# A two-layer transformer trunk in f32: index scores and attention logits as three rounded terms, and a reordered end

## The reference

```python
sc = einsum('bqhd,bsd->bqhs', qi, ki)              # 8 index heads of 64, one shared key
I = einsum('bqh,bqhs->bqs', wi * idx_scale, relu(sc))
vals, idx = lax.top_k(where(adm, I, -inf), 64)     # 64 keys for each query
logits = einsum('bqhd,bqkhd->bqhk', q, k[idx]) * 0.125
prob = softmax(where(valid, logits, -inf)); out = einsum(prob, v[idx])
```

## Time and profile before

| | |
|---|---|
| median of 3 runs (1175.69 to 1175.87) | 1175.69 us |
| profiled execution, own time | 1175.69 us |
| its span | 1173.9 us |
| TensorE busy | 99% |
| VectorE, ScalarE, GpSimd busy | 70%, 52%, 10% |
| TensorE's granted clock over the span | 0.998 |

### The profile page before, as it was taken

One profiled execution on the slowest core, in us unless ns is written; L12 is line 12 of the kernel. 1 busy time (PEld: TensorE's weight loads), 2 busy tenths in 40 slices (PEclk: granted clock), 3 DMA queues, 4 the chain that ended last, 5 costly groups with the idle time before them and its releaser, 6 DMA issues.

```text
span 1173.9 us, 24028 instructions
## 1 busy us (share of the span) xinstructions
PE 1166.0 (99%) x10518; PEld 1142.5 (97%) x10518; DVE 820.7 (70%) x936; ACT 610.0 (52%) x689; POOL 117.3 (10%) x130
## 2 busy tenths in 40 slices
PE   9999999999999999999999999999999999999998
PEld 9999999999999999999999999999899999999997
DVE  6866545697978766655786665458799787666556
ACT  6544445555745644444764443447466555444455
POOL 2000001011512000001110000100134020000011
PEclk9999999999999999999999999999999999999999
DMA  8655555545445555555546555554644456655551
GB/s 296 230 203 189 190 204 176 188 150 204 152 145 194 202 193 201 191 188 196 192 179 220 184 205 186 184 213 141 218 146 149 140 207 210 203 184 201 190 180 37
DMA packets 33528, 218.87 MB, mean 186 GB/s; under 512 B 5200, under 2 KB 6544, under 8 KB 7440
## 3 DMA queue, kind: packets, MB, share of 16 engines
q1 hardware_dynamic: 33424, 217.34, 53.5%
HBM read 216.15 MB, written 1.05 MB: 185 GB/s over the span
## 4 chain that ended last, share of the span: by engine, by line
PE 98%; DMA 1%; DVE 0%; ACT 0%; SPq 0%; DVEq 0%; issue 0%
PE psum L408 32%; PE psum L409 31%; PE psum L410 31%; PE psum L690 1%; PE psum L669 1%; DMA x_all<-in_x 1%; PE psum L542 0%; PE psum L603 0%; PE psum L653 0%; PE psum L724 0%; DVE gates L1795 0%; PE psum L638 0%; PE psum L735 0%; PE psum L758 0%; DVE hB_lo L1763 0%; PE psum L585 0%
## 5 line engine op out<-in xcount | busy, mean ns | idle before, releaser
L1303 DVE TENSOR_TENSOR w_lo<-raw,w_hi 128x2048 fp32r<-128x2048 f32 x200 | 457.9, 2293 | 218.7 <-ACT w_hi L903 218.5
L903 ACT ACTIVATE w_hi<-raw 128x2048 fp32r<-128x2048 f32 x201 | 385.2, 1916 | 352.2 <-PE psum L410 344.3
L408 PE MATMUL psum<-hA_hi,w_hi 128*128 128x256 f32 x1360 | 377.6, 278 | 0.0
L409 PE MATMUL psum<-hA_hi,w_lo 128*128 128x256 f32 x1360 | 375.7, 276 | 0.0
L410 PE MATMUL psum<-hA_lo,w_hi 128*128 128x256 f32 x1360 | 375.6, 276 | 0.0
L408 PEld LDWEIGHTS psum<-hA_hi,w_hi 128*128 128x128 f32 x1360 | 255.3, 188 | 2.7 <-issue 2.7
L409 PEld LDWEIGHTS psum<-hA_hi,w_lo 128*128 128x128 f32 x1360 | 255.3, 188 | 0.0
L410 PEld LDWEIGHTS psum<-hA_lo,w_hi 128*128 128x128 f32 x1360 | 255.3, 188 | 0.0
L408 PE MATMUL psum<-hB_hi,w_hi 128*128 128x256 f32 x832 | 229.9, 276 | 1.0 <-DVE w_lo L1771 1.0
L409 PE MATMUL psum<-hB_hi,w_lo 128*128 128x256 f32 x832 | 229.7, 276 | 0.0
L410 PE MATMUL psum<-hB_lo,w_hi 128*128 128x256 f32 x832 | 229.7, 276 | 0.0
(11 more groups left out here) (208 smaller groups left out, 1240.7 us busy)
## 6 DMA issues: line engine op xcount, KB each, us to landing
raw<-in_weights SPq DMA_DIRECT2D x203, 1024.0 KB, 4.9
raw<-in_weights SPq DMA_DIRECT2D x2, 512.0 KB, 6.2
out<-gates SPq DMA_DIRECT2D x4, 192.0 KB, 2.2
x_all<-in_x SPq DMA_DIRECT2D x1, 520.0 KB, 3.9
x_all<-in_x SPq DMA_DIRECT2D x1, 512.0 KB, 6.3
relu<-in_p SPq DMA_DIRECT2D x2, 256.0 KB, 5.0
consts<-in_consts SPq DMA_DIRECT2D x1, 384.0 KB, 5.6
out<-gates SPq DMA_DIRECT2D x2, 128.0 KB, 2.0
```

Of the source, the lines that this page charges most:

```text
L408: pe.matmul(o, lh, rh, start=start, stop=False)
L409: pe.matmul(o, ll, rh, start=False, stop=False)
L903: act.activation(w_hi[:, s, :], raw[:, s, :], ACT.Copy).then_inc(hi_ready[s], 1)
L1303: dve.tensor_tensor(w_lo[:, s, :], raw[:, s, :], w_hi[:, s, :].bitcast(F32), ALU.subtract).then_inc(lo_ready[s], 1)
```

## The change

It does three things. (1) The index scores are computed as three rounded terms, `iq_hi x ik_hi`, `iq_lo x ik_hi`, `iq_hi x ik_lo`, in the same places of the array, and the logits as `q_hi x k_hi`, `q_lo x k_hi`, `q_hi x k_lo`, with all 128 queries at once (64 x 128 of the array, as the scores, not 64 x 64). (2) The rounded parts come from ScalarE and the rests from VectorE. (3) At the end the ones products, the fillers and the stores are reordered and the root of a constant is removed.

```diff
-WARM_BEFORE_SUMS = 3
+WARM_BEFORE_SUMS, WARM_BEFORE_SPREAD = 1, 2
@@ SP, end; the odd stores are ScalarE's
+                    if (t * len(STORES) + i) % 2 == 0:
+                        sp.wait_ge(out_ready, t * len(STORES) + i + 1)
+                        sp.dma_start(out[:, t, tiles, :], final[:, t, tiles, :]).then_inc(stored, 16)
@@ TensorE, scores
+                        for term, (q, key) in enumerate(((iq_hi, ik_hi), (iq_lo, ik_hi), (iq_hi, ik_lo))):
+                            for r in range(2):
+                                rows = slice(64 * r, 64 * r + 64)
+                                mm = pe.matmul(bank[BANK_OF[f"sc{j + r}"]][:, i * nk:(i + 1) * nk], q[rows, 2 * m + i, qt * P:(qt + 1) * P],
+                                               key[rows, 0:nk], start=term == 0, stop=term == 2)
@@
-                pe.wait_ge(keys_copied, (L + 1) * 16)
+                pe.wait_ge(ik_lo_ready, (L + 1) * 2)
@@ TensorE, logits
-                            for c in range(2):
-                                at = qt * P + 64 * c
-                                mm = pe.matmul(bank[BANK_OF[f"lg{j + r}"]][64 * c:64 * c + 64, i * nk:(i + 1) * nk],
-                                               qT[rows, 2 * m + i, at:at + 64], kT[rows, 2 * m + i, 0:nk], start=True, stop=True)
+                        for term, (q, key) in enumerate(((q_hi, k_hi), (q_lo, k_hi), (q_hi, k_lo))):
+                            for r in range(2):
+                                rows = slice(64 * r, 64 * r + 64)
+                                mm = pe.matmul(bank[BANK_OF[f"lg{j + r}"]][:, i * nk:(i + 1) * nk], q[rows, 2 * m + i, qt * P:(qt + 1) * P],
+                                               key[rows, 2 * m + i, 0:nk], start=term == 0, stop=term == 2)
@@ TensorE, ahead of logits(0)
-                        for name in ("aq1", "ak1"):
-                            wait_drained(pe, L, name)
+                        wait_drained(pe, L, "aq1")
+                        pe.wait_ge(k_lo_ready, (L + 1) * 2)
@@ TensorE, end
+            pe.wait_ge(x_done, (L_N - 1) * 16 + 15)
+            pe.wait_ge(last_squares, 1)
+            for t in range(2):
+                add_tile(1, t)
+            pe.wait_ge(sq_added, of_norm(L_N, 0, 3) + START)
+            for t in range(2):
+                add_tile(0, t)
             keep_warm(WARM_BEFORE_SUMS)
...
             for t in range(2):
                 pe.wait_ge(last_squares, 2 + t)
                 add_tile(2, t).then_inc(sums_done, 1)
+            keep_warm(WARM_BEFORE_SPREAD)
@@ ScalarE; the copies of iq, aq0 and aq1 write iq_hi and q_hi
+                        act.wait_ge(keys_copied, (L + 1) * 16)
+                        for rows, at in copied:
+                            act.activation(ik_hi[rows, :], ikT[rows, at, :], ACT.Copy).then_inc(ik_hi_ready, 1)
@@ after split(L, MIX + 14)
+                for i in range(2):
+                    wait_drained(act, L, f"ak{i}")
+                    act.activation(k_hi[:, 2 * i:2 * i + 2, :], iqT[:, 2 * i:2 * i + 2, :], ACT.Copy).then_inc(k_hi_ready, 1)
@@ end
-                    act.activation(rsum[:, 0, 0:1], eps, ACT.Sqrt)
@@ VectorE
+                def rest_of_bank(ready, hi, lo, name, i):
+
+                    dve.wait_ge(ready, L * 2 + i + 1)
+                    dve.tensor_tensor(lo[:, 2 * i:2 * i + 2, :], two_tiles(name), hi[:, 2 * i:2 * i + 2, :].bitcast(F32), ALU.subtract
+                                      ).then_inc(drained[BANK_OF[name]], 1)
+
                 split(L, MIX + 6)
+                rest_of_bank(iq_hi_ready, iq_hi, iq_lo, "iq0", 0)
+                for i, (rows, at) in enumerate(((slice(0, 64), 1), (slice(64, 128), 0))):
+                    dve.wait_ge(ik_hi_ready, L * 2 + i + 1)
+                    dve.tensor_tensor(ik_lo[rows, :], ikT[rows, at, :], ik_hi[rows, :].bitcast(F32), ALU.subtract).then_inc(ik_lo_ready, 1)
+                rest_of_bank(iq_hi_ready, iq_hi, iq_lo, "iq1", 1)
                 split(L, MIX + 7)
@@
                 distance(64, 63)
+                rest_of_bank(q_hi_ready, q_hi, q_lo, "aq0", 0)
                 split(L, MIX + 11)
+                rest_of_bank(q_hi_ready, q_hi, q_lo, "aq1", 1)
                 top_k(L, 1, halfway=take_first_keys)
                 chunk_products(L, AK + 1)
-                take(L, "ak1", kT[:, 2:4, :])
+                take(L, "ak1", iqT[:, 2:4, :])
                 split(L, MIX + 13)
                 split(L, MIX + 14)
+                for i in range(2):
+                    dve.wait_ge(k_hi_ready, L * 2 + i + 1)
+                    dve.tensor_tensor(k_lo[:, 2 * i:2 * i + 2, :], iqT[:, 2 * i:2 * i + 2, :], k_hi[:, 2 * i:2 * i + 2, :].bitcast(F32),
+                                      ALU.subtract).then_inc(k_lo_ready, 1)
                 split(L, MIX + 15)
```

More of the change, by code:

```diff
@@ L141, in hybrid_trunk @@
         pT_hi_, pT_lo_ = (b[:, 2, :].rearrange("p (k t) -> p k t", t=T) for b in (small_hi, small_lo))
+        iq_hi, iq_lo = oa_hi, oa_lo
+        q_hi, q_lo = obT_hi, obT_lo
+        ik_hi, ik_lo = (b[:, :, :].rearrange("p a t -> p (a t)") for b in (diag_hi, diag_lo))
         zg = silu
@@ L174, in hybrid_trunk @@
         prob = sb("prob", [P, 2, 512])
-        qT = sb("qT", [P, 4, T])
+        k_hi = sb("k_hi", [P, 4, T], F32R)
         sb("after_qT", [P, BEFORE_HB])
@@ L178, in hybrid_trunk @@
         ikT = sb("ikT", [P, 2, T])
-        kT = sb("kT", [P, 4, T])
+        k_lo = sb("k_lo", [P, 4, T], F32R)
         v = sb("v", [P, 2, 512])
@@ L227, in hybrid_trunk @@
         keys_copied = sem("keys_copied")
+        ik_hi_ready = sem("ik_hi_ready")
+        ik_lo_ready = sem("ik_lo_ready")
+        iq_hi_ready = sem("iq_hi_ready")
+        q_hi_ready = sem("q_hi_ready")
+        k_hi_ready = sem("k_hi_ready")
+        k_lo_ready = sem("k_lo_ready")
         p_landed = sem("p_landed")
@@ L392, in _ @@
                 for i, tiles in enumerate(STORES):
-                    sp.wait_ge(out_ready, t * len(STORES) + i + 1)
-                    sp.dma_start(out[:, t, tiles, :], final[:, t, tiles, :]).then_inc(stored, 16)
+                    if (t * len(STORES) + i) % 2 == 0:
+                        sp.wait_ge(out_ready, t * len(STORES) + i + 1)
+                        sp.dma_start(out[:, t, tiles, :], final[:, t, tiles, :]).then_inc(stored, 16)
             sp.wait_ge(stored, 16 * 2 * len(STORES))
@@ L531, in chunk, with scores @@
                     return s
-                def scores(qT_, kT_, name, j):
+                def scores(j):
                     qt, _, m = STEPS[j]
@@ L537, in scores @@
                     for r in range(2):
-                        wait_free(pe, L, f"{name}{j + r}")
+                        wait_free(pe, L, f"sc{j + r}")
                     for i in range(2):
[L540 to L545, removed]
+                        for term, (q, key) in enumerate(((iq_hi, ik_hi), (iq_lo, ik_hi), (iq_hi, ik_lo))):
[3 more added lines that the diff above has]
+                                               key[rows, 0:nk], start=term == 0, stop=term == 2)
+                                if i and term == 2:
+                                    done(mm, f"sc{j + r}")
                 for t in range(2):
@@ L576, in mix @@
                         wait_drained(pe, L, f"iq{j // 2}")
-                    scores(iqT, lambda rows, hp, nk: ikT[rows, 0 if rows.start else 1, 0:nk], "sc", j)
+                    scores(j)
                 chunk(GQ, "gq")
@@ L598, in logits @@
                     for i in range(2):
-                        for r in range(2):
-                            rows = slice(64 * r, 64 * r + 64)
-                            for c in range(2):
-                                at = qt * P + 64 * c
-                                mm = pe.matmul(bank[BANK_OF[f"lg{j + r}"]][64 * c:64 * c + 64, i * nk:(i + 1) * nk],
-                                               qT[rows, 2 * m + i, at:at + 64], kT[rows, 2 * m + i, 0:nk], start=True, stop=True)
-                            if i:
-                                done(mm, f"lg{j + r}")
+                        for term, (q, key) in enumerate(((q_hi, k_hi), (q_lo, k_hi), (q_hi, k_lo))):
[3 more added lines that the diff above has]
+                                               key[rows, 2 * m + i, 0:nk], start=term == 0, stop=term == 2)
+                                if i and term == 2:
+                                    done(mm, f"lg{j + r}")
                 for n, c in [(GV, "gv"), (GR, "gr")]:
@@ L866, in _ @@
             pe.wait_ge(pgate_scaled, L_N * 4 - 1)
-            keep_warm(WARM_BEFORE_SUMS)
-            pe.wait_ge(sq_added, of_norm(L_N, 0, 3) + START)
             def add_tile(c, t):
                 return pe.matmul(bank[SUM_BANKS[t]][:, T:T + 1], last_squared[:, c - 1, HALVES[t]] if c else total[:, HALVES[t]], ones[:, 0:1],
-                                 start=c == 0, stop=c == 2)
+                                 start=c == 1, stop=c == 2)
```

(28 more changed lines are left out.)

## The result

| | before | after |
|---|---|---|
| median | 1175.70 us (4 runs, 1175.69 to 1175.87) | 1190.76 us (4 runs, 1190.62 to 1191.12) |
| ratio | | 1.0128, 95% interval 1.0116 to 1.0141 |
| span of the profiled run | 1173.9 us | 1189.0 us |
| mean granted clock of TensorE | 0.998 | 0.994 |

The change made the kernel 15.1 us slower. The forecast was 1185.6 with a range to 1190.2; the time lies 0.6 us above the range. The sign and the places were right. What failed is the choice that TensorE's clock holds while it waits.

What follows compares the result with a forecast made beforehand. The prediction took TensorE to bound the kernel. From 1175.7 us it added 10.1 for both layers (5.06 each: 4.42 at the first logits, 0.64 at the others) and took off 0.2 at the end: 1185.6 us, range 1183.4 to 1190.2.

Steps and rivals of the forecast that it cites:

- What bounds the kernel: The chain that ended last lies on TensorE for 98%, so each microsecond it stands or works longer is the kernel's.
- The price of a rounded pair: On TensorE, a pair of rounded products (two heads, 64 x 128) takes 0.11 us for 128 and 256 columns.
- rivals of slow, serial or faster pairs: Rounded pairs on TensorE: slow 1188.2 or serial 1190.9 us, chance 8%; faster weight loads 1184.3 us, chance 9%.
- Scores: Index scores in each layer: no gain from the products, start 0.5 us late for `ik_lo`, end 0.6 us late.
- The rests of q and k: Before `logits(0)`: VectorE's added rests make `k_lo` late, TensorE stands 3.6 us, GR's first product comes 4.42 us later.
- The other logits: Logits calls of j = 2, 4 and 6: +0.48 us, then +0.08 each, together +0.64 a layer.
- The end: Reordered products and stores at the kernel's end: -0.2 us, between -0.35 and +0.3.
- The clock: Wait before `logits(0)`: the sum had TensorE's clock hold; the rival, 27%, had it fall, giving 1187.3 or 1189.0 us.
- The other side: Rival, chance 3%: before `logits(0)` the rests are ready in time and products pay by columns alone; 1172.9 us.

Runs made afterwards that it cites:

- the filled kernel: The changed kernel with 17 products of ones on TensorE ahead of its wait for `k_lo`; 1186.30 us, ratio 1.0089.
- half-filled kernel: The changed kernel with 9 products of ones on TensorE ahead of its wait for `k_lo`; 1187.90 us.
- e7: The kernel before with rounded logits alone, `logits(0)` behind GR's first chunk, a plain copy of q by ScalarE, all rests behind split 47; 1177.15 us.
- quarter filling: The changed kernel with 4 products of ones on TensorE ahead of its wait for `k_lo`; 1190.58 us.
- rests first: The changed kernel with VectorE's two rests of k ahead of splits 46 and 47 instead of behind them; 1180.75 us, ratio 1.0042.

## Why the prediction was wrong, by its steps

- **What bounds the kernel** was right: every loss but the 0.15 us at the end lies on TensorE's path.
- **The price of a rounded pair**, 0.11 us for 128 and 256 columns, was right (0.11 and 0.12). The rivals of slow, serial or faster pairs are out. By the fast weight load of the Trainium skill ("TensorE: Matmul & The Clock Gate", "Weight-path perf modes"), were it in force for the rounded type, pairs of 128 columns could have come about 0.055 apart, an estimate from the factor of about 2 that the section gives as measured; the rows show 0.11.
- **Scores**: forecast 0.6 late with a wait of 0.5; measured 0.69 and 0.72 with 0.54. Right.
- **The rests of q and k**: forecast a stand of 3.6 us and +4.42 at GR, scores included. Measured 3.85 and 3.77; without the clock's share, by the filled kernel, 0.69 + 4.11 = 4.80 and 0.72 + 4.05 = 4.77. Right in kind, 0.4 short in each layer: VectorE reached the copy of `ak1` at 261.01, not 260.42. Of these 0.6 us, 0.17 are the later start of the whole kernel, 0.14 came at the scores and 0.3 in the first top-k, where the forecast took its list as unmoved.
- **The other logits**: forecast 0.48 and twice 0.08; measured 0.39 and next to nothing.
- **The end**: forecast -0.2. The multiplications did start 0.17 sooner, but in the profiled run the whole took 0.15 longer; alone it moves nothing that can be measured in the time. From the start of the last projection product to the end of the span it takes 8.87 us before, 8.68 or 8.69 in the three kernels with the new end and f32 logits, and 8.99 to 9.06 in the six with the new end and both rounded products. So the 0.15 is no chance of one trace; why the stores land later in those kernels stays open.
- **The clock: the failed step.** The sum stood on TensorE keeping 2.4 GHz through a stand of 3.6 us, since dense work lies on both sides. It didn't: 4.4 us. I had this as a rival with 27%, and priced a fall at 3.4 us of half speed, once a wait, 1.7 us each; the first fall held for 6.8 and cost 2.80, the second cost 1.57. All other terms together give 15.1 - 4.4 = 10.7, against 9.9 forecast. With the measured price the rival's time would have been 1175.7 + 9.9 + 4.4 = 1190.0. The Trainium skill ("TensorE: Matmul & The Clock Gate", "Why this matters for your kernels") warns of idle gaps between bursts of matmuls, and the trace agrees: with both stands of 3.8 us came the low level. The half-filled kernel shows it for a stand of 1.8 us too, in three runs of four. That is a shorter gap than the page warns of, and the measurement decides.
- **The other side** needed `k_lo` 3.6 us sooner. `e7` took the wait away by another way, with the logits later, and they still lost 0.25 at j = 0 and 0.39 at j = 2: products don't pay by columns alone.

**Left open.** Why the first fall lasts twice as long as the second in both traces that have two (the kernel after and the quarter filling), and why a stand of 3.0 us costs as much as one of 3.9. The five falls in the traces have one thing in common: the two that lasted 6.8 us began while TensorE still stood (at 266.7 and 266.9), the three that lasted 3.4 us when it was at work again (at 853.8, 854.0 and 268.2, the last in the half filling). No run tests whether that is the cause. The 0.17 us at the start of the kernel are -0.02 to 0.19 in the traces of the experiments and weren't followed up. No run has rounded products on 64 x 64 of the array, so the price of the new change of partition isn't shown by itself.

## What to carry to other kernels

Price a rounded product by its weights: three passes with 128 moving columns, each under a floor of 0.11 us for 128 weight columns, cost more than one f32 product in four places of the array. When a change adds operands made by a busy engine, put them in that engine's list where it has idle time, and the product behind them on the bound engine as late as its readers allow: moving one call gave back 10.6 of 15.1 us, 4.4 of it clock. And count a new stand of the matmul engine twice, once as time and once as clock.

## What was not expected of the hardware

- A stand of 3.0 to 3.9 us at two places cost 4.4 us of clock, and the eight runs with such stands took 1190.5 to 1191.1 us; one of 1.8 us cost 1.7 in three runs of four and nothing in one; one of 1.1 us (rests first) nothing.
- The clock came down inside the first stand, at 266.7, and 0.3 us after the end of the second one, at 853.8, when TensorE was already at work. In the half filling it came down at 268.2, 0.9 us after the stand.
- At 1.2 GHz a rounded pair of 128 columns took 0.21 us and at 2.4 GHz 0.11, so the floor of 0.11 us a pair goes with the clock.
